# Prompt attention of a two-layer decoder: both maps transposed at once, scores as three 64-row products in two halves of the array, 1024-wide pieces

## The reference

```
qs = q.reshape(bsz, tq, h, 2, DIFF_DH)      # DIFF_DH = 64
ks = k.reshape(bsz, tk, h, 2, DIFF_DH)
s = einsum('bqhmd,bkhmd->bhmqk', qs, ks) * DIFF_DH ** -0.5
s = s + rel_bias[t5_bucket(rel)]            # by distance; constant from 128 on
s = where(rel >= 0, s, finfo.min)
p = softmax(s)
a = p[:, :, 0] - lam * p[:, :, 1]
o = einsum('bhqk,bkhd->bqhd', a, v)         # v has 128 dimensions per head
```

## Time and profile before

| what | us |
|---|---|
| median of 3 runs (lowest, highest) | 4095.71 (4092.16, 4099.85) |
| span of the profiled execution, first to last instruction | 4093.1 |
| PE / DVE / ACT busy in the whole span | 3702.2 / 1841.7 / 1162.0 |
| prompt attention, from its first DMA to its end | 2293 to 3187, 894 long |
| in it, PE / DVE / ACT busy | 769.70 / 748.02 / 581.20 |

### The profile page before, as it was taken

The page is one execution under the profiler, slowest core; times in us unless marked ns, Lnnn a source line. Parts: engine busy times, 40 slices in busy tenths (PEclk is TensorE's granted clock), DMA queues, the critical chain, the costliest instruction groups (busy, mean ns, idle before and its releaser), DMA issues. The chain is left out here.

```text
span 4093.1 us, 57158 instructions
## 1 busy us (share of the span) xinstructions
PE 3702.2 (90%) x19551; PEld 3035.2 (74%) x19551; DVE 1841.7 (45%) x4144; ACT 1162.0 (28%) x1916; POOL 119.0 (3%) x156
## 2 busy tenths in 40 slices
PE   5999897995999989998999688888889799869999
PEld 4888796773888868887888577777777667458887
DVE  2222211555555531113222388888888222165554
ACT  2111111332222120102111266666666211121111
POOL 0000001110000000000000000000000000000000
PEclk9999998997999989999999899999999899879999
DMA  4211322336222231213212622222210546242221
GB/s 143 72 67 67 112 89 85 114 112 223 79 74 87 72 131 67 72 69 144 74 64 69 133 57 51 53 64 64 64 33 12 199 170 219 97 173 72 86 82 49
DMA packets 305344, 385.23 MB, mean 94 GB/s; under 512 B 153574, under 2 KB 211719, under 8 KB 305175
## 3 DMA queue, kind: packets, MB, share of 16 engines
q1 hardware_dynamic: 305174, 383.18, 28.9%
HBM read 278.63 MB, written 104.47 MB: 94 GB/s over the span
## 5 line engine op out<-in xcount | busy, mean ns | idle before, releaser
L234 PE MATMUL vg_ps_y<-vg_w_hi,vg_x_hi 128*128 128x512 f32 x1088 | 428.0, 393 | 10.9 <-ACT vg_w_hi L263 10.9
L236 PE MATMUL vg_ps_y<-vg_w_lo,vg_x_hi 128*128 128x512 f32 x1088 | 425.0, 391 | 0.0
L238 PE MATMUL vg_ps_y<-vg_w_hi,vg_x_lo 128*128 128x512 f32 x1088 | 424.8, 390 | 0.0
L1506 PE MATMUL att_ps_o<-att_v,att_a_t 128*128 128x128 f32 x2176 | 296.1, 285 | 51.0 <-ACT att_a_t L1567 50.6
L1506 PEld LDWEIGHTS att_ps_o<-att_v,att_a_t 128*128 128x128 f32 x2176 | 278.0, 197 | 76.0 <-ACT att_a_t L1567 53.2
L1634 DVE TENSOR_SCALAR_CACHE_REDUCE att_s<-att_ps_s,att_far 128x512 f32<-128x512 f32 (+3 forms) x608 | 326.6, 582 | 6.0 <-PE att_ps_s L1479 1.9
L1555 ACT ACTIVATE att_s<-att_s,att_neg 128x128 f32<-128x128 f32 (+15 forms) x256 | 307.2, 1200 | 2.7 <-DVE att_neg L1651 2.1
L1478 PE MATMUL att_ps_s<-att_k_hi,att_q_hl 128*128 128x512 f32 (+3 forms) x640 | 260.8, 414 | 11.7 <-DVE att_s L1634 10.8
L234 PEld LDWEIGHTS vg_ps_y<-vg_w_hi,vg_x_hi 128*128 128x128 f32 x1088 | 205.3, 189 | 53.3 <-issue 11.7
L238 PEld LDWEIGHTS vg_ps_y<-vg_w_hi,vg_x_lo 128*128 128x128 f32 x1088 | 205.2, 189 | 43.0
L236 PEld LDWEIGHTS vg_ps_y<-vg_w_lo,vg_x_hi 128*128 128x128 f32 x1088 | 205.3, 189 | 41.6
(11 more groups left out here) (269 smaller groups left out, 6431.2 us busy)
## 6 DMA issues: line engine op xcount, KB each, us to landing
smp_k_pg<-in_cache_k SPq DMA_DIRECT2D x64, 512.0 KB, 5.1
smp_v_pg<-in_cache_v SPq DMA_DIRECT2D x64, 512.0 KB
factors<-vg_out SPq DMA_DIRECT2D x68, 256.0 KB, 2.0
res_factors<-factors SPq DMA_DIRECT2D x34, 512.0 KB
res_o<-mixer_out SPq DMA_DIRECT2D x34, 512.0 KB, 4.4
att_k_nat<-out_k SPq DMA_DIRECT2D x128, 128.0 KB, 2.7
att_q_nat<-diff_q SPq DMA_DIRECT2D x128, 128.0 KB, 3.0
gla_x<-gla_qka SPq DMA_DIRECT2D x17, 520.0 KB, 3.4
```

The source lines that it names most:

```text
L234: nc.tensor.matmul(ps_y[g][:, 0:width[g]], x_hi[u][:, k, :], w_hi[:, k, cols], start=(k == 0), stop=False)
L236: nc.tensor.matmul(ps_y[g][:, 0:width[g]], x_hi[u][:, k, :], w_lo[:, k, cols], start=False, stop=False)
L238: mm = nc.tensor.matmul(ps_y[g][:, 0:width[g]], x_lo[u][:, k, :], w_hi[:, k, cols], start=False, stop=(k == KD - 1))
L1506: mm = nc.tensor.matmul(ps_o[:, 0:D_VD], a_t[n % 2][:, (b % 4) * P:(b % 4 + 1) * P], v_sb[u][:, b, :], start=(b == 0), stop=(b == i))
```

## The change

The two maps lie side by side as they are in HBM, so that one transposed unit has map 0 in partitions 0 to 63 and map 1 in 64 to 127: 8 units for a head, one in every even tile, 2 DMAs for a group. High and low parts are separate tensors. A piece of scores is three products of 64 rows for each map (high x high, high x low, low x high), maps alternating, each in its half of the array. Pieces are up to 1024 keys wide (two banks), in three slots; both maps of a piece are announced together. `ps_a` is one bank, shared by `prep` and `turn`. Scores have the opposite sign, so that DVE keeps a minimum that is the exponential's bias as it stands and `neg` goes; for that `setup` writes a second, negated table of biases.

```diff
 def key_pieces(n):
-    ends = list(range(n, 0, -BANK))
-    return [(max(0, e - BANK), e) for e in reversed(ends)]
+    ends = list(range(n, 0, -2 * BANK))
+    return [(max(0, e - 2 * BANK), e) for e in reversed(ends)]
...
-    RING = 4
-    preps = [(is_q, m, g) for g in range(4) for m in range(2) for is_q in (False, True)]
+    SLOTS = 3
+    preps = [(is_q, g) for g in range(4) for is_q in (False, True)]
+    prep_of = [i // 2 if i % 2 == 0 else None for i in range(T)]
...
-        ps_s = [ps(f"ps_s{i}") for i in range(RING)]
-        ps_k = ps("ps_k")
-        ps_a = [ps(f"ps_a{i}") for i in range(2)]
+        ps_s = [ps(f"ps_s{i}", 2 * BANK) for i in range(SLOTS)]
+        ps_a = ps("ps_a")
...
                 def scores(H, u, i):
...
+                        pe.wait_ge(s["piece_free"], after(PIECES * H + n + 2))
+                        for at in range(lo_, hi_, BANK):
+                            end = min(at + BANK, hi_)
+                            for q_part, k_part in ((q_hi, k_hi), (q_hi, k_lo), (q_lo, k_hi)):
+                                for m in range(2):
+                                    rows = slice(m * D_DH, (m + 1) * D_DH)
+                                    mm = nc.tensor.matmul(ps_s[(n + m) % SLOTS][:, at - lo_:end - lo_],
+                                                          q_part[u][rows, i * P:(i + 1) * P],
+                                                          k_part[u][rows, at:end],
...
+                        mm.then_inc(s["piece_ready"], 1)
+                        yield
+                def turn(H, i, g, prepped):
...
+                    pe.wait_ge(s["a_copied"], after(GROUPS * H + first_group[i] + g))
...
+                        if prepped is not None:
+                            pe.wait_ge(s["a_copied"], after(GROUPS * H + first_group[i]))
+                            prep(H + 1, prepped, own_bank[0])
+                        coming = scores(*ahead(H, u, i, 2)) if not (last and i + 2 >= T) else iter(())
+                        next(coming, None)
+                        turn(H, i, 0, prepped)
+                        next(coming, None)
+                        for g in range(1, groups[i]):
+                            turn(H, i, g, prepped)
+                            meet(H, u, i, g - 1)
+                        meet(H, u, i, groups[i] - 1)
...
             def _(dve):
...
                             take(*ahead(H, u, i, 1))
+                        if not last and prep_of[i] is not None:
+                            low(H + 1, 1 - u, prep_of[i], own_bank[0])
                         combine(H, u, i)
...
+                for dst, src in ((rev, row), (rev_neg, row_neg)):
+                    sp.dma_start(dst, src[:, :].rearrange("h (a m) -> h a m", a=1).broadcast_to([D_HEADS, P, REV])
+                                 ).then_inc(stored, 16)
+                sp.wait_ge(stored, after(32))
```

More of the change, by code:

```diff
@@ L1325, in attention @@
     NEAR = 2 * P
+    HEAD_SCALE = -(D_DH ** -0.5)
     pieces = [key_pieces((i + 1) * P) for i in range(T)]
@@ L1387, in over_heads, with need_head @@
             head(D_HEADS - 1, 1, True)
-        def slots(i):
-            start = sum(beside[:i])
-            return preps[start:start + beside[i]], start
+        def need_head(H, u):
+            return 48 * (H // 2 + 1) if isinstance(H, int) else 24 * (H - u) + 48
         core.begin()
@@ L1449, in _, with prep @@
             def _(pe):
[L1450 to L1456, removed]
+                def prep(H, n, bank):
+                    is_q, g = preps[n]
+                    if not is_q:
+                        pe.wait_ge(nat_in[g], after(32 * (H + 1)))
@@ L1464, in scores @@
                 def scores(H, u, i):
[L1466 to L1478, removed]
-                            nc.tensor.matmul(dst, lhs, k_lo[u][m][:, lo_:hi_], start=False,
-                                             stop=True).then_inc(s["piece_ready"], 1)
-                            yield
@@ L1623, in take @@
                     near = max(0, n_keys - NEAR)
-                    for m in range(2):
-                        col = 0
-                        for c, (lo_, hi_) in enumerate(pieces[i]):
-                            n = first_piece[i] + m * len(pieces[i]) + c
-                            dve.wait_ge(s["piece_ready"], after(PIECES * H + n + 1))
-                            if m == 0 and c == 0:
-                                dve.wait_ge(s["max_done"], after(T * H + i))
-                            cut = min(hi_, near)
+                    col = 0
@@ new lines, in take @@
+                    for c, (lo_, hi_) in enumerate(pieces[i]):
+                        n = first_piece[i] + 2 * c
+                        cut = min(hi_, near)
+                        start = max(lo_, near)
+                        dve.wait_ge(s["piece_ready"], after(PIECES // 2 * H + n // 2 + 1))
+                        if c == 0:
+                            dve.wait_ge(s["shift_done"], after(T * H + i))
+                        for m in range(2):
+                            bank, at = ps_s[(n + m) % SLOTS], col
@@ L1646, in take @@
-                                col += 1
+                                    out=s_sb[i % 2][:, m, start:hi_], in0=bank[:, start - lo_:hi_ - lo_],
+                                    in1=bias[u][:, NEAR - (n_keys - start):NEAR], scale=1.0, scalar=3.0e38,
+                                    op0=ALU.add, op1=ALU.min, accum_out=low_of[:, m, at:at + 1])
+                                at += 1
                             ins.then_inc(s["piece_free"], 1)
-                    dve.wait_ge(s["piece_free"], after(PIECES * H + first_piece[i + 1] + RING))
@@ L1673, in head @@
                             take(*ahead(H, u, i, 1))
+                        if not last and prep_of[i] is not None:
+                            low(H + 1, 1 - u, prep_of[i], own_bank[0])
                         combine(H, u, i)
-                        if not last:
-                            for n, (is_q, m, g) in enumerate(slots(i)[0]):
-                                low(H + 1, 1 - u, slots(i)[1] + n, is_q, m, g)
-                dve.sem_inc(s["piece_free"], RING)
-                for n, (is_q, m, g) in enumerate(preps):
-                    low(0, 0, n, is_q, m, g, turn_banks)
+                for n in range(PREPS):
+                    low(0, 0, n, first_banks[n % len(first_banks)])
+                dve.wait_ge(s["lo_done"], after(PREPS))
+                dve.sem_inc(s["piece_free"], SLOTS)
                 take(0, 0, 0)
```

173 lines of the change are left out of this document (75 added, 98 removed).

## The result

The changed kernel takes 4282.44 us (median of four, 4275.66 to 4287.88), the kernel before 4096.93 beside it: 1.045 times as long, 95% interval 1.044 to 1.047, +185.5 us. The forecast was +94.

The account below looks back on a forecast made before the run. DVE was taken to set the pace in prompt attention. Seven heads +71, last head +6, start -14 and setup +31 made +94 on 4095.7, so 4190 us; range 4085 to 4310.

Parts of the forecast that it names:

- favoured case: Whole kernel: tables one after the other, halves side by side, chain as walked; 4190 us, 4150 to 4235, chance 0.47.
- rival in which the halves run one after the other: Score products on PE: the two maps' half-array products do not overlap; +102 us, 4292, chance 0.20.
- setup: Bias tables: the second, negated table transfers behind the first on the same DMA engines; +31 us.
- start of the stage: Prompt attention, first DMA to first take: 11 DMAs ahead instead of 35, 12 us instead of 26.4; -14 us.
- seven heads with units: Prompt attention: seven heads that prepare units, each +10.2 us; +71 us.
- last head: Prompt attention, head without units: only the wait for scores remains, less savings in small tiles; +6 us.
- wait for scores: Tiles 7 to 14: three slots delay PE's second piece; DVE stands still about 1 us in each two-piece tile.
- Beside the first on the idle engines: Setup: the second table transfers side by side with the first at no cost; 4159 us, chance 0.12.
- change between half-array and full-height products: PE tiling mode: no cost in the sum; by the skill's drain rule 0.17 us each, 22 us, left out.
- new chain in even tiles: Even tiles: `a` waits for exponential, copies, meets, unit, high, low; tile 12 takes 11.9 us against 8.95.
- sum for a head: One head with units: tiles 7 to 14 +12.4 us, tiles 15 and 0 to 6 -2.2; together +10.2 us.
- rival in which DVE's saving arrives: Heads: PE and ACT steps overlap more, DVE stays the bound and saves 12.8 us each; 4016 us, chance 0.16.

Follow-up runs that it names:

- run 2: Changed kernel with both bias tables written by one DMA from sixteen partitions in setup; 4248.66 us.
- Run 1: Changed kernel with only `low` moved behind `combine`, as before the change; 4139.39 us, 1.0105 times the kernel before.
- run 6: As 4, but with `low` ahead of `combine`, as in the changed kernel; 4192.43 us.
- 4: Changed kernel with 512-wide pieces, four score banks, own unit bank, two `ps_a`, earlier mixing, `low` behind `combine`; two tables still; 4066.49 us, 0.9926 times before.
- run 3: Changed kernel with six unused full-height 512-wide products added per tile on PE, ahead of the first turn; 4267.81 us.
- run 5: As 4, with one DMA for both bias tables; 4034.9 us, 0.9854 times the kernel before.
- run 12: Changed kernel with `low` behind `combine`, one table DMA, 512-wide pieces in four banks, own unit bank, two banks for `a`, PE's order kept; 4108.79 us.
- run 7: Changed kernel with three products of map 0, then three of map 1 for each bank, instead of alternating; 4281.03 us.

## Why the prediction was right in its direction and half the size

The direction, the place and each mechanism were as forecast; one term of the sum, that of the heads, was mis-sized, so the time lies above the 4150 to 4235 that the favoured case had. It lies close to the 4292 of the rival in which the halves run one after the other, and that is chance: the rows show a pair every 0.23 us.

| term | forecast | measured |
|---|---|---|
| setup | +31 | +31.45 in the profile, of which run 2 takes back 29.5 there |
| start of the stage | -14 | 26.4 to 15.2 (2330.04 to the first take at 2345.26): -11 |
| seven heads with units | +71 | 926.2 against 769.5: +157 |
| last head | +6 | 97.0 against 88.8: +8 |

- **Setup, start, halves, wait for scores** held. The products ran side by side (0.23 us for a pair), which was the lower of the two bounds. The forecast of about 1 us of standstill for scores is seen where the clock is full (0.99 in the mean of 38 second pieces). "Beside the first on the idle engines" did not happen. The change between half-array and full-height products, which the sum put at nothing, shows 0.10 us for a step in one direction (last section).
- **The new chain in even tiles** held for the large ones almost to the tenth: walked 8.6, 10.25, 11.9 and 13.65 for tiles 8, 10, 12 and 14, measured 8.9, 10.3, 11.85 and 13.9 (means of seven heads, end of `a` to end of `a`). Run 1, and run 6 against 4, show that `low` ahead of `combine` is its condition: 143 and 126 us.
- **The step that failed in size** is the sum for a head, +10.2, measured +22 (157 over 7). Walked 118.7 for a head, it took 132.3. The base was a little short too: the head of 108.5 was one of the quicker ones, the seven took 109.9 in the mean. Half of the missing 14 us is in tiles 0, 2, 4 and 6 (walked 8.4, 4.4, 5.3, 6.55; measured 10.3, 6.1, 8.05, 7.6), a third in tiles 7, 9, 11 and 13 (7.2, 7.5, 8.1, 8.8 became 8.2, 8.45, 9.1, 10.1), tile 15 adds 0.9. The odd tiles' part is TensorE's clock, which the forecast named and left unpriced: run 3 brought them back to the walk, and 24 of the 26 second pieces that came at a lower clock fall into the periods of these tiles; at 1.2 us each (2.20 less 0.99) that is 29 us, and over the seven heads these tiles took 30 more than walked. In tile 4 the rows show some 1.5 us of it. How much of the small even tiles is the clock in all wasn't separated: with the clock at 0.98 they fell only in part (tile 4 to 6.9, tile 0 not at all).
- **What stands against it.** DVE's saving is real: with `low`, PE's order and the banks as before (run 5) the seven heads take 717.2 us against 769.5, 7.5 less for a head. The forecast had 12.8, of which 4.4 are for wide pieces, which run 5 doesn't have. So the rival in which DVE's saving arrives comes near a kernel that exists, with `low` and PE's order where they were; the changed one isn't it.
- **The turn of group 1 behind the second piece**, which the forecast put into E, has its nearest size from run 12 to 5: 74 us, on the ring of four and with `low` behind; up to three pieces stand ahead of group 1 there, in the changed kernel one of 1024. What it costs in the changed kernel by itself was not measured.

## What to carry to other kernels

An instruction that consumes a late product of another engine belongs behind the one that the next step waits for; moved ahead of it, it put two engines' queues in order into the path here and cost 126 to 143 us, with either set of banks. When work is saved on the engine that sets the pace, look at the order on the engines that feed it first: with the order, pieces and banks of before and one DMA for the tables, the saving that was left made the kernel 1.5% faster instead of 4.5% slower. A walk along a chain at full-clock prices comes out short if the chain leaves TensorE idle: here 14 us of 132 for a head, of which run 3 ties at least 4 (the odd tiles) to the clock.

## What the runs showed of the hardware that was not expected

- Products of the two halves ran as pairs even with three of one map ahead of three of the other (run 7: the second pair of a bank starts 0.34 us after the first, as it does in the changed kernel, and the third 0.23 after that). The pairing does not need alternating instructions at this distance.
- Where 64-row products are followed by full-height ones, the step is 0.33 us (2718.73 to 2719.06 in the changed kernel, a 512-wide pair to a turn whose `a` had ended at 2718.20) instead of 0.23 to 0.24 between full-height ones of that width and the next (2615.36 to 2615.60 before). The Trainium skill, "TensorEngine Tiling (Array Packing)", Key Properties, says that a change of mode drains TensorE. The rows show 0.10 us more in this direction, where the forecast had named an estimate of 0.17 for each; that the drain makes them, and what it costs in all, no run tests by itself.
- Behind 2.58 us without work on PE, the granted clock from 2709.50 to 2712.50 was 0.50 (1.2 GHz), and a pair of 512-wide products took 0.43 us there instead of 0.23.
